# Two edits in a long fused kernel: the order of the scan's output matmuls, and the branch inputs split in fours with their sigmoids tile by tile

## What is computed

```python
# h: normalised input; ug: its 1024 scan columns in 64 groups of 16; 64 states a group
x_re, x_im = complex_scan(ab, coef * (b @ ug))         # along the 256 tokens
y = c_re @ x_re - c_im @ x_im + d_skip * ug            # per group
y = gelu(y)
ssm  = y * sigmoid(y @ w_glu + b_glu)                  # 1024 columns
attn = attention(q, k, v)                              # 8 heads, 1024 columns
g1, g2 = sigmoid(gates)                                # 2 x 2048 columns of the same projection
merged = g1 * (attn @ w_attn_br) + g2 * (ssm @ w_ssm_br)
x = x + gate * (merged @ w_out)
```

## Time and profile before

| | before |
|---|---|
| median of 3 runs | 3751.93 us |
| the profiled execution's own time | 3747.92 us |
| its span | 3746.3 us |
| PE matmul busy | 3612.7 us (96%) |
| DVE busy | 2572.4 us (69%) |
| ACT busy | 2113.1 us (56%) |
| POOL busy | 71.1 us (2%) |
| mean DMA rate | 192 GB/s |

### The profile page before, as it was taken

The page is one execution under the profiler, slowest core; times in us unless marked ns, Lnnn a source line. Parts: engine busy times, 40 slices in busy tenths (PEclk is TensorE's granted clock), DMA queues, the critical chain, the costliest instruction groups (busy, mean ns, idle before and its releaser), DMA issues.

```text
span 3746.3 us, 75816 instructions
## 1 busy us (share of the span) xinstructions
PE 3612.7 (96%) x26600; PEld 3390.2 (90%) x26600; DVE 2572.4 (69%) x4815; ACT 2113.1 (56%) x3811; POOL 71.1 (2%) x137
## 2 busy tenths in 40 slices
PE   7999998999999999999999989999988899999998
PEld 6999998999999999787888879889988899999998
DVE  5775647788877777555688868887656666666555
ACT  4446644666667776454555555554554566666453
POOL 1000000000000000000000000000000000000000
PEclk9999999999999999999999999999999999999999
DMA  7854457555554444566788844444444455555554
GB/s 262 313 195 148 149 197 286 187 178 178 176 178 161 159 162 152 173 212 213 269 330 331 328 157 139 154 132 143 148 154 157 148 185 179 182 186 183 175 185 153
DMA packets 183888, 721.09 MB, mean 192 GB/s; under 512 B 20416, under 2 KB 22976, under 8 KB 170688
## 3 DMA queue, kind: packets, MB, share of 16 engines
q1 hardware_dynamic: 166464, 608.57, 48.2%
q0 software_dynamic: 14352, 102.77, 7.6%
q10 hardware_dynamic: 2928, 7.83, 0.6%
HBM read 714.89 MB, written 4.19 MB: 192 GB/s over the span
## 4 chain that ended last, share of the span: by engine, by line
PE 90%; DVE 5%; ACT 2%; issue 1%; DMA 1%; ACTq 0%; DVEq 0%; SPq 0%
PE PS L394 22%; PE PS L396 21%; PE PS L395 21%; PE PS L526 6%; PE PS L527 6%; PE PS L528 6%; PE PS L730 1%; PE PS L779 1%; DVE wlo L1296 1%; ACT whi L900 1%; DVE big L1364 1%; PE PS L539 0%; PE PS L422 0%; PE PS L606 0%; DVE big L1784 0%
## 5 line engine op out<-in xcount | busy, mean ns | idle before, releaser
L900 ACT ACTIVATE whi<-raw 128x512 fp32r<-128x512 f32 x2296 | 1425.0, 629 | 1440.9 <-PE PS L396 1084.8
L1296 DVE TENSOR_TENSOR wlo<-raw,whi 128x512 fp32r<-128x512 f32 x2296 | 1538.3, 690 | 994.5 <-ACT whi L900 981.4
L394 PE MATMUL PS<-hhi,whi 128*128 128x256 f32 (+1 forms) x6976 | 1992.5, 286 | 83.4 <-DVE hlo L1355 21.6
L395 PE MATMUL PS<-hlo,whi 128*128 128x256 f32 (+1 forms) x6976 | 1969.5, 282 | 0.0
L396 PE MATMUL PS<-hhi,wlo 128*128 128x256 f32 (+1 forms) x6976 | 1969.1, 282 | 0.0
L394 PEld LDWEIGHTS PS<-hhi,whi 128*128 128x128 f32 x6976 | 1323.8, 190 | 111.9 <-issue 71.1
L396 PEld LDWEIGHTS PS<-hhi,wlo 128*128 128x128 f32 x6976 | 1324.3, 190 | 0.0
L395 PEld LDWEIGHTS PS<-hlo,whi 128*128 128x128 f32 x6976 | 1320.6, 189 | 0.6
L526 PE MATMUL PS<-whi,hhi 128*128 128x512 f32 x1024 | 404.3, 395 | 4.8 <-issue 3.6
L527 PE MATMUL PS<-wlo,hhi 128*128 128x512 f32 x1024 | 404.3, 395 | 0.0
L528 PE MATMUL PS<-whi,hlo 128*128 128x512 f32 x1024 | 404.1, 395 | 0.0
(11 more groups left out here) (400 smaller groups left out, 2251.2 us busy)
## 6 DMA issues: line engine op xcount, KB each, us to landing
raw<-peer_u_dram SPq DMA_DIRECT2D x256, 512.0 KB, 3.3
raw<-peer_v_dram SPq DMA_DIRECT2D x256, 512.0 KB, 4.3
raw<-w_in_dram SPq DMA_DIRECT2D x240, 512.0 KB, 4.1
big<-w_mod_dram POOLq DMA_DIRECT2D x96, 1024.0 KB, 5.2
raw<-w_up_dram SPq DMA_DIRECT2D x176, 512.0 KB, 3.3
raw<-w_down_dram SPq DMA_DIRECT2D x88, 512.0 KB, 3.3
raw<-w_out_dram SPq DMA_DIRECT2D x64, 512.0 KB, 3.3
raw<-w_query_dram SPq DMA_DIRECT2D x32, 512.0 KB, 4.9
```

The source lines that it names most:

```text
L394: pe.matmul(out, hi, rhi, start=start, stop=False, **more)
L395: pe.matmul(out, hi, rlo, start=False, stop=False, **more)
L900: f(whi[:, m % PAIRS, quarter(q)], raw[:, m % RING, quarter(q)], ACT.Copy).then_inc(hi_ready, 1)
L1296: dv.tensor_tensor(wlo[:, m % PAIRS, quarter(q)], raw[:, m % RING, quarter(q)], whi[:, m % PAIRS, quarter(q)], ALU.subtract).then_inc(lo_r ...
```

## The change

There are two edits.

In `read_out` the loops change places: the terms k are outside, the four blocks q inside. The matmuls are the same 16.

In the branches:
- The 32 gate tiles get a sigmoid each (`open_gate`): four behind the last four tiles of `w_glu`, the others by twos in the first 14 tiles of `w_attn_br`. `gates_open` counts tiles.
- The product of y and `glug` goes by four tiles, in DVE's turns 1 and 2 of `w_attn_br`; its high parts come in ACT's turns 4 and 5, its low parts in DVE's turns 6 and 7.
- `h2b` is split by four tiles, inside `w_ssm_br`: `merged_high` on ACT ahead of the weight pairs 2, 4 and 6 of its loop (and one behind it), `merged_low` on DVE in turns 6, 10 and 14 (and one behind). The second eight tiles go to new places, `mhi` and `mlo`, over tiles 8 to 23 of `p2`, which are free by then.
- `w_out_2` waits for its input group by group in its first tile. `SPLITS` is renumbered.
- DVE's and ACT's loops over `w_attn_br` and `w_ssm_br` are written out instead of run as loops of the engine.

```diff
-SPLITS = {"h": 4, "merged": 8, "h2": 12, "h3": 16, "ys0": 17, "ya": 18, "ys": 19, "m2": 21, "h4": 25}
+SPLITS = {"h": 4, "merged": 8, "h2": 12, "h3": 16, "ys0": 17, "ya": 18, "ys": 20, "m2": 24, "h4": 28}
...
-                                             hhi[:, half * 8 + kc, o:], hlo[:, half * 8 + kc, o:],
+                hi, lo = (hhi[:, half * 8:, o:], hlo[:, half * 8:, o:]) if halves is None else halves[half]
...
-                for q in range(4):
-                    for k, (part, of) in enumerate(((0, ta), (2, tb), (1, q_), (1, p))):
+                for k, (part, of) in enumerate(((0, ta), (2, tb), (1, q_), (1, p))):
+                    for q in range(4):
                         last = pe.matmul(PS[32 * q:32 * q + 32, 6, 0:SEQ], cc[:, part, 4 * n + q, :], of[:, q, :],
                                          start=k == 0, stop=k == 3)
...
-            pe.wait_ge(in_ready, SPLITS["m2"])
-            dense_and_squares("w_out_2", 320, None, sqb, squares_end)
+            dense_and_squares("w_out_2", 320, SPLITS["ys"], sqb, squares_end,
+                              ((hhi[:, 8:, META:], hlo[:, 8:, META:]), (mhi, mlo)))
...
+            def open_gate(n):
+
+                f(p2[:, 32 + n, :], p2[:, 32 + n, :], ACT.Sigmoid).then_inc(gates_open, 1)
...
-            for half in range(2):
-                f(p2[:, 32 + 16 * half:48 + 16 * half, :], p2[:, 32 + 16 * half:48 + 16 * half, :],
-                  ACT.Sigmoid).then_inc(gates_open, 1)
-
-            split_only("w_attn_br", 8)
-            split_input(SPLITS["ya"], p2[:, 24:32, :], 0, 8, META)
-            split_only("w_ssm_br", 8)
-            split_input(SPLITS["ys"], h2b, 0, 8, META)
+                if k >= 4:
+                    open_gate(k - 4)
+            for k in range(16):
+                for n in (2 * k + 4, 2 * k + 5):
+                    if n < 32:
+                        open_gate(n)
+                if k % 2 == 0:
+                    split(0, FIRST["w_attn_br"], k + 2)
+                if k in (4, 5):
+                    part = slice(4 * (k - 4), 4 * (k - 4) + 4)
+                    sc.wait_ge(in_f32, SPLITS["ya"] + k - 3)
+                    f(hhi[:, part, META:], p2[:, 24 + 4 * (k - 4):28 + 4 * (k - 4), :], ACT.Copy).then_inc(in_hi, 1)
+
+            def merged_high(q):
+
+                sc.wait_ge(in_f32, SPLITS["ys"] + q + 1)
+                to = hhi[:, 8 + 4 * q:12 + 4 * q, META:] if q < 2 else mhi[:, 4 * q - 8:4 * q - 4, :]
+                f(to, h2b[:, 4 * q:4 * q + 4, :], ACT.Copy).then_inc(in_hi, 1)
+
+            for k in range(8):
+                if k in (2, 4, 6):
+                    merged_high(k // 2 - 1)
+                split(0, FIRST["w_ssm_br"], 2 * k + 2)
+            merged_high(3)
...
+            for k in range(16):
+                if k % 2 == 0:
+                    split(0, FIRST["w_attn_br"], k + 2)
+                if k in (1, 2):
+                    part = slice(24 + 4 * (k - 1), 28 + 4 * (k - 1))
+                    dv.wait_ge(banks_free, 4 + 288)
+                    dv.tensor_tensor(p2[:, part, :], p2[:, part, :], glug[:, 4 * (k - 1):4 * k, :], ALU.mult).then_inc(in_f32, 1)
+                if k in (6, 7):
+                    part = slice(4 * (k - 6), 4 * (k - 6) + 4)
+                    dv.wait_ge(in_hi, SPLITS["ya"] + k - 5)
+                    dv.tensor_tensor(hlo[:, part, META:], p2[:, 24 + 4 * (k - 6):28 + 4 * (k - 6), :], hhi[:, part, META:],
+                                     ALU.subtract).then_inc(in_ready, 1)
+                dv.wait_ge(quarters_used, 2 * (PAIRS + FIRST["w_attn_br"] + k + 1))
+                dv.wait_ge(gates_open, k + 1)
+                dv.tensor_tensor(h2b[:, k, :], PS[:, k % 4, 0:SEQ], p2[:, 32 + k, :], ALU.mult).then_inc(banks_free, 1)
...
+            for k in range(16):
+                if k % 2 == 0:
+                    split(0, FIRST["w_ssm_br"], k + 2)
+                if k in (6, 10, 14):
+                    merged_low((k - 6) // 4)
+                dv.wait_ge(quarters_used, 2 * (PAIRS + FIRST["w_ssm_br"] + k + 1))
+                dv.wait_ge(gates_open, 16 + k + 1)
+                dv.tensor_tensor(mtmp[:, k % 2, :], PS[:, k % 4, 0:SEQ], p2[:, 48 + k, :], ALU.mult).then_inc(banks_free, 1)
+                dv.wait_ge(banks_free, 4 + 304 + k + 1)
+                i = dv.tensor_tensor(h2b[:, k, :], h2b[:, k, :], mtmp[:, k % 2, :], ALU.add)
+                if k % 4 == 3:
+                    i.then_inc(in_f32, 1)
+                    dv.wait_ge(in_f32, SPLITS["ys"] + k // 4 + 1)
+                else:
+                    link(i)
+            merged_low(3)
```

More of the change, by code:

```diff
@@ L217, in build @@
         glug = region(B2, 8, SEQ)
+        mhi = nc.alloc_sbuf_tensor_at("mhi", [P, 8, SEQ], F32R, offset=at_big + 4 * 8 * SEQ)
+        mlo = nc.alloc_sbuf_tensor_at("mlo", [P, 8, SEQ], F32R, offset=at_big + 4 * 16 * SEQ)
         mtmp = region(B2 + 2048, 2, SEQ)
@@ L405, in dense, with dense_and_squares @@
                     dense_turn(name, chunk0, width, g)
-            def dense_and_squares(name, chunk0, inputs, of, ready):
+            def dense_and_squares(name, chunk0, inputs, of, ready, halves=None):
                 def one_sum(n):
@@ L414, in dense_and_squares @@
                     dense_turn(name, chunk0, SEQ, g, lambda k: one_sum(4 * g + k - 1) if g + k > 0 else None,
-                               inputs if g == 0 else None)
+                               inputs if g == 0 else None, halves)
                 one_sum(KC - 1).then_inc(sums, 1)
@@ L429, in head_spread, with dense_turn @@
                           start=True, stop=True).then_inc(head_wide, 1)
-            def dense_turn(name, chunk0, width, g, after=None, inputs=None):
+            def dense_turn(name, chunk0, width, g, after=None, inputs=None, halves=None):
                 h0_ = FIRST[name]
@@ L445, in dense_turn @@
                                 at_ = slice(kc * P, (kc + 1) * P)
-                                last = three(PS[:, c, 0:width], whi[:, half, at_], wlo[:, half, at_],
-                                             hhi[:, half * 8 + kc, o:], hlo[:, half * 8 + kc, o:],
+                                hi, lo = (hhi[:, half * 8:, o:], hlo[:, half * 8:, o:]) if halves is None else halves[half]
+                                last = three(PS[:, c, 0:width], whi[:, half, at_], wlo[:, half, at_], hi[:, kc, :], lo[:, kc, :],
                                              half == 0 and kc == 0, half == 1 and kc == 7)
@@ L1902, in _ @@
                 split(0, FIRST["w_glu"], 2 * k + 2)
[L1904 to L1911, removed]
@@ L1912, in _ @@
-            dv.wait_ge(banks_free, 4 + 304)
[L1913 to L1924, removed]
@@ L1925, in _ @@
-            dv.memset(small[:, 26:27], 0.0).then_inc(in_f32, 2)
-            split_input(SPLITS["ys"], h2b, 0, 8, META)
+            for k in range(16):
[13 more added lines that the diff above has]
+                dv.tensor_tensor(h2b[:, k, :], PS[:, k % 4, 0:SEQ], p2[:, 32 + k, :], ALU.mult).then_inc(banks_free, 1)
@@ new lines, in _, with merged_low @@
+            dv.wait_ge(banks_free, 4 + 304)
+            def merged_low(q):
+                hi, lo = (t[:, 8 + 4 * q:12 + 4 * q, META:] if q < 2 else m[:, 4 * q - 8:4 * q - 4, :]
+                          for t, m in ((hhi, mhi), (hlo, mlo)))
+                dv.wait_ge(in_hi, SPLITS["ys"] + q + 1)
+                dv.tensor_tensor(lo, h2b[:, 4 * q:4 * q + 4, :], hi, ALU.subtract).then_inc(in_ready, 1)
+            for k in range(16):
[13 more added lines that the diff above has]
+                    link(i)
```

## The result

The changed kernel takes 3713.76 us in the median of 4 runs (3709.57 to 3716.40), the kernel before beside it 3751.42 (3750.18 to 3752.04). The ratio is 0.9899 with a 95% interval of 0.9883 to 0.9915, so 37.7 us less where 40.3 were forecast, inside the range. The profiled execution is one of 3713.97 us, its span 3712.4.

The account below looks back on a forecast made before the run. PE, busy 96% of the span, bounds the kernel. Read_out's 21.0 us plus the branches' net 19.3 (25.9 removed, 6.6 added) make 40.3, so 3751.93 falls to 3711.6 us, range 3704 to 3726.

Parts of the forecast that it names:

- Four streams over all 128 partitions: In read_out, four column blocks start together, each reading all 128 partitions, which no row showed; 2.10 us a call.
- sign of a shared port: In read_out, records longer than 0.38 would show the forecast wrong, through a shared read port.
- the upper bound: Read_out's gain lies between 0 and the full 21.0 us; the full one was taken.
- A: Rival in read_out: the array feeds only two column blocks at once, 3.78 us a call, 3725.0 in all; chance 0.08.
- B: Rival in read_out: the order gives nothing and only the branches count, 3732.6 us; chance 0.06.
- C: Rival in read_out: each change of column block drains the array, slower, about 3796 us; chance 0.04.
- DVE's cover: Behind each read_out DVE's 2.19 us idle lets PE's gain arrive; without it at most 3.6 us lost.
- What was removed from the branches: Holes of 2.09, 9.27 and 10.48 us, with clock losses of 2.0 and 2.1, go: together -25.9.
- What was added: In the branches, new waits at w_attn_br, w_ssm_br and w_out_2: together +6.6 us, leaving net -19.3.
- The holes of `w_ssm_br`: PE stalls of 0.3, 1.45 and 1.45 us while ACT waits for DVE's sums: +3.2.
- The hole of `w_out_2`: Inside its first tile PE waits for the fourth group's low part: +2.85 us.
- no fall of the clock: Behind w_out_2's 2.85 us hole the clock was taken to stay up; a drop would cost 2.1 us.

Follow-up runs that it names:

- e2: The changed kernel with read_out's loops put back in the old order: 3734.8 us, ratio 0.9957.
- e3: The changed kernel with read_out's blocks taken two at a time, 0 and 1 alternating, then 2 and 3: 3717.7 us, ratio 0.9917.
- e4: The changed kernel with ACT's first three high parts of the merged input one pair of weights later in w_ssm_br: 3714.1 us, ratio 0.9901.
- e6: The changed kernel with mhi and mlo laid out as hhi and hlo, 272 columns a tile read from the 17th: one execution, 3710.5 us.
- e5: The kernel of e4 with DVE's third low part ahead of the last weight split of w_ssm_br: one execution, 3709.7 us.
- e10: The changed kernel itself, unaltered, measured once more on the same chip: 3714.75 us, ratio 0.9899.
- e1: The kernel before with the change of read_out's loops alone: 3727.8 us, ratio 0.9942.

## Why the prediction was right

**The bound.** PE's chain decided, as read: nearly every microsecond taken from PE arrived.

**Read_out.** Forecast 2.10 a call and 21.0 in all; measured 2.07 and 21.3. The difference is that the four starts lie closer together than L768's. Four streams over all 128 partitions were the unknown; the pitch within a block is 0.216 us as before. (The records' length, 379 ns in the median before and after, says little, since the profile models their ends; so the prediction's sign of a shared port, records longer than 0.38, was a weak one.) The "9 start" of its reading of the earlier trace rows are 8, which changes no term. The choice of the upper bound rested on reading the overlap already there as look-ahead, and the two-by-two order confirms it. Rivals A, B and C asked for 3.8, 4.7 and over 7 us. The Trainium skill's rule in "TensorE: Matmul & The Clock Gate" (Part 3), that with equal row groups no weight load overlaps a matmul, doesn't hold here: 16 weight loads and 12 matmul records start in 0.60 us. Its 2.38x for three column tiles (given for 512 columns; the prediction calls it an example of another data type, but the page's table names none) is the better guide: this call's 32 records would take 7.1 us in a row and take 1.93.

**DVE's cover.** The 2.19 idle is gone and the scan's later holes in PE are the same within 0.05 us; nothing of the gain was lost.

**What was removed from the branches.** `w_attn_br` -11.5 against -11.2 and `w_ssm_br` -9.7 against -9.3: the sizes of holes and low stretches, read from the earlier trace rows, were right.

**What was added.** By its stages the second edit brought 17.3 us (the median of e2 says 16.0) where 19.3 were forecast. Three terms were mis-sized, in part against each other, 1.8 us in all:
- The holes of `w_ssm_br` were forecast at 0.3, 1.45 and 1.45. There are two of 1.2 and none at the first group. The step was the length of DVE's two products and sums, 2.2 us from the earlier trace rows. Written out, a product follows a sum 0.46 us later in place of 0.58, and the four take 1.8 (rows below). So the 0.8 less lies in the edit's unrolling, which I had put at nothing; the unrolled loop was not run by itself.
- The hole of `w_out_2` was forecast at 2.85 and is 2.6, for the same reason. The step that failed is the one behind it: no fall of the clock, from the one row of a 2.50 idle without one. All six traces that have this hole (the changed kernel's two, and those of e2, e3, e4 and e6) have 3.4 us of low clock behind it, 1.7 lost. Behind the 2.1 idle ahead of `w_attn_br` it fell in four of nine (e2, e4, e5, e10), and behind the 2.50 idle of the earlier trace rows, which all twelve traces have, in one (e2). Behind the idles of 1.8 and 1.9 of before and e1 and the 1.4 of e5 it did not fall. So a hole between 2 and 3 us is not safe here, and one row without a fall proves nothing.
- `w_out_2`'s pitch, +1.1, was not in the sum at all: I had counted the new places of the input as free.

DVE's last operations of a pair of tiles, in the kernel before and in the changed one:

```profile
2844.36 0.43 DVE L1924 TENSOR_TENSOR big<-big 128x256 f32 x1 [0.17 <-DVE big L1921]
2844.94 0.43 DVE L1921 TENSOR_TENSOR big<-PS,big 128x256 f32<-128x256 f32 x1 [0.15 <-DVE big L1924]
...
2797.42 0.42 DVE L1959 TENSOR_TENSOR big<-big 128x256 f32<-128x256 f32 x1
2797.88 0.42 DVE L1957 TENSOR_TENSOR big<-PS,big 128x256 f32<-128x256 f32 x1
```

**The scatter.** The stretch ahead of `w_in_2`, whose code all twelve traces share, takes 2238.7 to 2245.5 us, with 40 to 61 us of low clock, the most in the longest ones; the executions of one kernel scatter by some 7 us alike. So single totals a few microseconds apart say little here.

## What to carry to other kernels

Matmuls that use only 32 columns of the array ran beside each other here when they went to different blocks, but only as far as the look-ahead reached in program order (4.73 us a call one by one, 2.07 in turn): let the blocks take turns, and put the accumulation outside. When a long stretch of one engine is cut up and spread between another engine's feeds, ask for each piece what it waits for at that place: a piece that waits holds the feeds queued behind it, and one turn later it cost nothing here (e4). What remains is the chain behind the last tile; take from it all that could have been done earlier, and count a hole of more than 2 us with the fall of the clock, 1.7 us here.

## What the hardware showed that I had not expected

- Four fp32 streams of 128 partitions by 32 columns ran side by side, each at the 0.216 us pitch of a single one: 32 records in 1.93 us.
- The same fp32r matmul starts every 116.9 to 120 ns depending on where its moving input lies in SBUF (619 against 612 records in 75 us), and moving one half of the input changed the pitch of the other half as well. The cause is open.
- The clock fell to its lower level, for 3.4 us, after PE idles as short as 2.1 us, in some executions and not in others of the same kernel.
